# A two-layer transformer and a hybrid layer in one kernel: other SBUF addresses for the weight ring and the attention outputs

## The reference

```python
for l in range(2):
    proj = rmsnorm(x, attn_norm_g[l]) @ w_in[l]          # 2048 -> 4032 columns
    qa, ka, va, ga, cq, ckv, kr, gb = split(proj)
    ya = swa_attention(qa, ka, va, sinks) * silu(ga)     # 16 heads of 64, window 128
    yb = mla_attention(cq, ckv, kr, w_q_b, w_kv_b) * silu(gb)   # 8 heads of 128
    x = x + concat(ya, yb) @ w_out[l]                    # 2048 x 2048
x = rmsnorm(x)
hs = concat(16 meta tokens, x)
q, k, v, g_attn, u, g_pool, m_attn, m_pool = split(rmsnorm(hs) @ w_in_2)   # 2048 -> 10240 columns
y_attn = (stick_breaking_attention(q, k, v) * silu(g_attn)) @ w_attn_up    # 8 heads of 128
y_pool = (multiscale_pool(u) mixed by pool_w * silu(g_pool)) @ w_pool_up
hs = hs + (sigmoid(m_attn) * y_attn + sigmoid(m_pool) * y_pool) @ w_out_2
return rmsnorm(hs)[without the meta tokens]
```

## Time and profile before

| | us |
|---|---|
| median of 2 runs | 2917.66 (2916.66 to 2918.66) |
| profiled execution | 2917.28 |
| its span, first to last instruction | 2915.6 |

### The profile page before, as it was taken

The page is one execution under the profiler, slowest core; times in us unless marked ns, Lnnn a source line. Parts: engine busy times, 40 slices in busy tenths (PEclk is TensorE's granted clock), DMA queues, the critical chain, the costliest instruction groups (busy, mean ns, idle before and its releaser), DMA issues.

```text
span 2915.6 us, 33754 instructions
## 1 busy us (share of the span) xinstructions
PE 2836.3 (97%) x13316; PEld 2323.9 (80%) x13316; DVE 1314.8 (45%) x1816; ACT 995.5 (34%) x1557; POOL 1091.3 (37%) x536
## 2 busy tenths in 40 slices
PE   7999999999999999999999999999999999999997
PEld 5888887778888888777887778788878888888886
DVE  6646555741455565474336444544334222222323
ACT  5233434522323334352333332333223233222321
POOL 3443332234444333213443333333444444444442
PEclk9999998999999999899999999999999999999998
DMA  5332231134433222213443222222222333336333
GB/s 160 101 110 71 67 116 42 45 106 137 139 99 120 70 73 73 92 38 85 137 145 87 73 73 73 73 73 77 82 91 94 114 122 115 109 113 206 115 130 108
DMA packets 307613, 288.11 MB, mean 99 GB/s; under 512 B 33152, under 2 KB 256000, under 8 KB 306944
## 3 DMA queue, kind: packets, MB, share of 16 engines
q1 hardware_dynamic: 300656, 263.93, 30.3%
q10 hardware_dynamic: 6800, 22.02, 2.0%
HBM read 259.66 MB, written 26.21 MB: 98 GB/s over the span
## 4 chain that ended last, share of the span: by engine, by line
PE 80%; DVE 12%; ACT 5%; issue 1%; POOL 1%; DMA 1%; DVEq 0%; SPq 0%; ACTq 0%
PE bank L828 23%; PE bank L830 22%; PE bank L829 22%; PE work L828 2%; DVE probs L1564 2%; PE work L830 1%; PE work L829 1%; PE o_bank L828 1%; PE work L1049 1%; PE o_bank L829 1%; PE o_bank L830 1%; DVE pt L1572 1%; DVE mixed L1136 1%; ACT w_hi L678 1%; DVE mixed L1135 1%
## 5 line engine op out<-in xcount | busy, mean ns | idle before, releaser
L819 POOL TENSOR_TENSOR w_lo<-w_raw,w_hi 128x1024 fp32r<-128x1024 f32 (+3 forms) x468 | 1002.5, 2144 | 1518.0 <-ACT w_hi L678 1518.0
L828 PE MATMUL bank<-act_in,w_hi 128*128 128x512 f32 x2664 | 1057.3, 397 | 27.2 <-DVEq L1223 13.5
L830 PE MATMUL bank<-act_in,w_lo 128*128 128x512 f32 x2664 | 1043.1, 392 | 0.0
L829 PE MATMUL bank<-act_in,w_hi 128*128 128x512 f32 x2664 | 1042.2, 391 | 0.0
L678 ACT ACTIVATE w_hi<-w_raw 128x1024 fp32r<-128x1024 f32 (+3 forms) x468 | 437.9, 937 | 1065.6 <-PE bank L830 632.0
L828 PEld LDWEIGHTS bank<-act_in,w_hi 128*128 128x128 f32 x2664 | 502.5, 189 | 135.8 <-POOL w_lo L819 19.0
L830 PEld LDWEIGHTS bank<-act_in,w_lo 128*128 128x128 f32 x2664 | 502.1, 188 | 108.0
L829 PEld LDWEIGHTS bank<-act_in,w_hi 128*128 128x128 f32 x2664 | 503.1, 189 | 99.5 <-issue 1.4
L828 PE MATMUL bank<-mixed,w_hi 128*128 128x512 f32 x768 | 300.1, 391 | 0.0
L830 PE MATMUL bank<-mixed,w_lo 128*128 128x512 f32 x768 | 299.3, 390 | 0.0
L829 PE MATMUL bank<-mixed,w_hi 128*128 128x512 f32 x768 | 299.3, 390 | 0.0
(11 more groups left out here) (247 smaller groups left out, 2915.9 us busy)
## 6 DMA issues: line engine op xcount, KB each, us to landing
w_raw<-in_w_in SPq DMA_DIRECT2D x512, 128.0 KB, 2.4
w_raw<-in_w_in SPq DMA_DIRECT2D x224, 256.0 KB, 2.9
w_raw<-in_w_out SPq DMA_DIRECT2D x64, 512.0 KB, 3.6
w_raw<-in_w_in SPq DMA_DIRECT2D x32, 512.0 KB, 3.7
w_raw<-in_w_out SPq DMA_DIRECT2D x64, 256.0 KB, 4.7
probs<-in_xT SPq DMA_DIRECT2D x32, 256.0 KB, 5.0
x_scr<-buf ACTq DMA_DIRECT2D x32, 256.0 KB, 3.0
probs<-x_scr SPq DMA_DIRECT2D x32, 256.0 KB, 5.0
```

Source lines behind the costliest of these rows:

```text
L819: nc.gpsimd.tensor_tensor(lo, raw, hi, ALU.subtract).then_inc(lo_ready, 1)
L828: pe.matmul(dst, lhs[0], rhs[0], start=start, stop=False, skip_group_check=skip)
L829: pe.matmul(dst, lhs[0], rhs[1], start=False, stop=False, skip_group_check=skip)
L830: return pe.matmul(dst, lhs[1], rhs[0], start=False, stop=stop, skip_group_check=skip)
```

## The change

It gives other addresses to tensors; every instruction stays as it is. `mixed` becomes a view that begins 16 bytes into a home 32 bytes larger; `x_fin` stays at the start of that home. The rings `w_hi` and `w_lo` become three tensors each. Small tensors that stood behind the big ones, and three gaps of 32 bytes, are put between the slots. All uses of the form `w_hi[:, c % RING, ...]` become `w_hi[c % RING][:, ...]`, in ScalarE's, GpSimd's and TensorE's code alike.

```diff
--- before.py
+++ after.py
@@ -292,13 +292,28 @@
 
         act_in = sb("act_in", [P, KT, 2, T], F32R)
         mixed_at = nc.sbuf_base
-        mixed = sb("mixed", [P, KT, 2, T], F32R)
+        mixed_home = sb("mixed", [P, KT * 2 * T + 8], F32R)
+        mixed = mixed_home[:, 4:4 + KT * 2 * T].rearrange("p (k s t) -> p k s t", k=KT, s=2)
 
         x_fin = nc.alloc_sbuf_tensor_at("x_fin", [P, KT, T], F32, offset=mixed_at)
         meta_in = sb("meta_in", [P, KT, 2, META], F32R)
         w_raw = sb("w_raw", [P, RAW, 2, T])
-        w_hi = sb("w_hi", [P, RING, 2, T], F32R)
-        w_lo = sb("w_lo", [P, RING, 2, T], F32R)
+        w_hi, w_lo = [None] * RING, [None] * RING
+        sinks = sb("sinks", [P, 2, 16])
+        sb("gap0", [P, 8])
+        w_hi[0] = sb("w_hi0", [P, 2, T], F32R)
+        r_meta = sb("r_meta", [P, META])
+        sb("gap1", [P, 8])
+        w_hi[1] = sb("w_hi1", [P, 2, T], F32R)
+        sinks8 = sb("sinks8", [P, 2, 16])
+        meta_acc = sb("meta_acc", [P, META])
+        w_hi[2] = sb("w_hi2", [P, 2, T], F32R)
+        w_lo[2] = sb("w_lo2", [P, 2, T], F32R)
+        fold = sb("fold", [2 * META, META])
+        w_lo[1] = sb("w_lo1", [P, 2, T], F32R)
+        stat = sb("stat", [P, 8, NB])
+        sb("gap2", [P, 8])
+        w_lo[0] = sb("w_lo0", [P, 2, T], F32R)
         pt = sb("pt", [P, 2, 1280], F32R)
         probs = sb("probs", [P, SB_COLS])
         probs2 = sb("probs2", [P, SB_COLS])
@@ -308,9 +323,6 @@
         sq = sb("sq", [P, T])
         acc = sb("acc", [P, T])
         acc2 = sb("acc2", [P, T])
-        r_meta = sb("r_meta", [P, META])
-        meta_acc = sb("meta_acc", [P, META])
-        fold = sb("fold", [2 * META, META])
         window = (probs[:, TM:2 * TM], probs2[:, TM:2 * TM])
         cos = sb("cos", [P, T])
         sin = sb("sin", [P, T])
@@ -323,9 +335,6 @@
         causal_r = sb("causal_r", [P, P], F32R)
         strict_r = sb("strict_r", [P, P], F32R)
         gains = sb("gains", [P, 114])
-        sinks = sb("sinks", [P, 2, 16])
-        sinks8 = sb("sinks8", [P, 2, 16])
-        stat = sb("stat", [P, 8, NB])
 
         bank = [ctx.enter_context(nc.psum_tensor(f"bank{i}", [P, T], F32)) for i in range(4)]
         work = [ctx.enter_context(nc.psum_tensor(f"work{i}", [P, T], F32)) for i in range(3)]
...
-                src, dst = w_raw[:, c % RAW, 0:nk, 0:w], w_hi[:, c % RING, 0:nk, 0:w]
+                src, dst = w_raw[:, c % RAW, 0:nk, 0:w], w_hi[c % RING][:, 0:nk, 0:w]
...
-                hi, lo = w_hi[:, c % RING], w_lo[:, c % RING]
+                hi, lo = w_hi[c % RING], w_lo[c % RING]
...
```

More of the change, by code:

```diff
@@ L809, in _ @@
                 raw = w_raw[:, c % RAW, 0:nk, 0:w]
-                hi = w_hi[:, c % RING, 0:nk, 0:w].bitcast(F32)
-                lo = w_lo[:, c % RING, 0:nk, 0:w]
+                hi = w_hi[c % RING][:, 0:nk, 0:w].bitcast(F32)
+                lo = w_lo[c % RING][:, 0:nk, 0:w]
                 if chunks[c][1] == "swa":
@@ L911, in meta_product @@
                     x = meta_in[:, kt, :, :].rearrange("p s t -> p (s t)")
-                    pe.matmul(work[0][0:2 * META, 0:256], x, w_hi[:, c % RING, kk, cols],
+                    pe.matmul(work[0][0:2 * META, 0:256], x, w_hi[c % RING][:, kk, cols],
                               start=first and kk == 0, stop=False, skip_group_check=True)
-                    ins = pe.matmul(work[0][0:META, 0:256], x[:, 0:META], w_lo[:, c % RING, kk, cols],
+                    ins = pe.matmul(work[0][0:META, 0:256], x[:, 0:META], w_lo[c % RING][:, kk, cols],
                                     start=False, stop=last and kk == 1, skip_group_check=True)
@@ L1096, in _ @@
                             cols = slice(128 * m, 128 * m + 128)
-                            ins = three(work[1 + m][:, :], (w_hi[:, c % RING, kk, cols], w_lo[:, c % RING, kk, cols]),
+                            ins = three(work[1 + m][:, :], (w_hi[c % RING][:, kk, cols], w_lo[c % RING][:, kk, cols]),
                                         (pooled[:, kk, 0], pooled[:, kk, 1]), kk == 0, kk == 1)
```

## The result

The changed kernel takes 2954.4 us (2953.6 and 2955.2) against 2917.66: ratio 1.0126, 95% interval 1.0082 to 1.0169. It is 37 us slower, where 24 us less were forecast.

A forecast was written before the change was run, and what follows sets the result against it. The prediction took the number of TensorE matmuls on the chain times the distance between two as the bound. Terms of -17 and -7 us from 2917.3 gave 2893 us, range 2832 to 2962.

The forecast's parts named there:

- The bound and its lever: TensorE's large matmuls: some 8600 on the chain, 13.5 ns each over the column stream, at most 116 us to gain.
- (a): Weight load beside moving operand act_in or mixed, 10,296 matmuls: -2 ns each for 8600 on the chain, -17 us.
- The slower rival: Matmul streams lock in at a worse phase: +4 to +8 ns, 2952 to 2986 us at all three slots; chance 0.21.
- its second place: The 16 bytes under mixed, putting slots at 176, 16 and 208 there: another place for a worse step, 2304 matmuls.
- The floor of 3 to 5 ns of overhead: 512-column matmuls with a load that costs nothing: 3 to 5 ns estimated, leaving at most 9.5 ns, -82 us.
- (b): Transients from 1550 to 2250 and in the two first layers: half taken away, -4 and -3 us.
- (c): Attention and other small products, some 1500: distances 0 and 128 cost the same, 0 us within +-3.
- (d): ScalarE and GpSimd writers of the ring: hidden behind a chunk of 5443 ns even if slower, 0 us.
- Nothing moves: Large matmuls: the 13.5 ns is a fixed price of changing weights, wherever they lie; 2912 to 2921 us; chance 0.24.
- The step falls away: Large matmuls: streams set apart no longer collide, distance 217 to 219 ns, 2821 to 2845 us; chance 0.17.

The follow-up runs named there:

- others_only: The kernel before with only pt, probs, buf and what follows, meta_in and w_raw moved as in the changed kernel; 2914.4 us, ratio 0.9986.
- all_slots_32: The kernel before with the whole ring 32 bytes on, so all three slots stand at 32; 2965.4 us, ratio 1.0168.
- meta_in_32: The kernel before with meta_in alone at 32, behind the ring; 2915.8 us, ratio 0.9995.

## Why the prediction was wrong

The bound and its lever were right. TensorE's step is what the time hangs on, and the addresses move it: from the lowest to the highest mean step of all kernels with whole loads (227.4 in `others_only`, 233.2 in `all_slots_32`) the time goes from 2914 to 2965 us, 8.8 us for each ns, near the 8.6 that 8600 matmuls on the chain gave. With the 4.1 ns that the step grew by, 8600 x 4.1 = 35 us, and 36.4 came.

The step that failed is (a), in sign: I took -2 ns "because it is the nearest row". The rows had one record of 387 ns and a mean of 232 ns over nine. To take the shortest record of a transient for a steady value had no ground; the steady step went up, by 4.1 ns in the mean. The mean of the transient, +5 ns, would have made 8600 x 5 = +43 us and been 6 us off. That nearness is luck in part: at 192 and 240 the step rose by 1.6 and 0.6 ns only, so three distances could also have given far less. I had written in the rival that the steady state was "already near the short end", and gave that 0.21. The slower rival named the place, the price (+4 to +8 ns, 2952 to 2986 us) and that the streams lock in, and holds, but for two things: slot 0 rose by 1.6 ns only, below its price, and its second place, the 16 bytes under `mixed`, costs nothing beside the ring's own distance. The floor of 3 to 5 ns of overhead, from which the sum took its lower bound, is shown by no run for 512 columns: no long stream stood closer than 226.7 ns.

(b) was wrong in kind. The three slots' distances are not seen to add a transient at each change of slot; each slot has a rhythm of its own from its first few matmuls on. The means from 1550 to 2250 are 398, 393 and 394 ns against 394, 391 and 391, a rise of 4, 2 and 3 ns, less than the 4 to 6 ns of the late stage. What did shorten the transients, in `meta_in_32`, is the place of `meta_in`, which (b) didn't name.

(c) read `v_sb` at 128 and `v_swa` at 0 as evidence that distance is nothing. For 512 columns 128 costs 4.8 ns (232.6 to 227.8). Rows in hundredths of a us over two or three matmuls among small products say little about steady streams. As a share of the time (c) was right: `others_only` is 0.14% below before.

(d) holds: 1058 ns for ScalarE and 2427 for GpSimd per chunk from 2500 to 2700 (1058 and 2411), and the wait for the ring grew with the chunk.

The two rival ends fail as well. "Nothing moves" held the 13.5 ns for a fixed price wherever the weights lie; the step went from 226.7 to 233.2 ns by nothing but the ring's place. "The step falls away" rested on collisions that distance 0 would make the worst; 0 is the best of thirteen. Its own sum, 2917 less 76 to 96 us, ends at 2841 and not at 2845.

The Trainium skill's "SBUF — State Buffer" (Who interferes with whom) gives TensorE two independent read ports and says that it never waits on anyone. The measurements disagree: by nothing but where one read stands relative to the other the step goes from 226.7 to 233.2 ns.

## What to carry to other kernels

In a stream of fp32r matmuls with a weight load each, let weights and moving operands start at the same place modulo 256 bytes (512 in the kernel before): of the distances tried none was clearly better, 240 cost nothing that the time could show (1.0003) and 32 cost 1.7%. The shares of busy time hardly show it (PE has 97% in both kernels), the step does. All this is one kernel's, with 512-column matmuls and 128-column loads. Read the distance between matmuls (count over a stretch without idle time) before and after any new allocation, also one that "only" adds a small tensor. When a trace shows a transient beside a steady state, its best member is no estimate of another steady state; its mean came near in this case, which is one case.

## What the hardware showed that I had not expected

- A dense stream holds steps such as 226.7, 228.3, 231.7, 233.3 and 236.7 ns for 100 us and more at one and the same clock, and two of them at one distance in one kernel.
- At the lower clock the distance costs nothing: 427 ns between starts (the median) before and in `all_slots_32` alike.
- Weight loads of 64 columns, with 64 output rows, at distance 0 put the matmuls 3.2 ns further apart than whole ones (229.9 against 226.7 ns).
- 64 bytes under all operands together change nothing (1.0003), 32 bytes under the weights alone 1.7%.
